# Rows of the scaled layer norm input 272 elements apart instead of 266, and four small tiles placed in the space before the split input

## The chip, the cores and the metric

The kernel runs on one core of a Trainium2 chip. The metric is the device time of one execution in microseconds. Before the change three timed runs took 1718.97, 1721.99 and 1723.23 us, a median of 1721.99 us.

## What is computed

One decoder layer for 256 prompt tokens and 8 sample tokens, which the kernel carries together as 264 columns (`TOK`). Cut to what matters here:

```
z = x @ w_in                                  # 2048 -> mixers and gates
m = sum_k sigmoid(gate_k(x)) * (branch_k @ w_branch[k])
x1 = LN(alpha*x + m @ w_out) * ln1_g + ln1_b
gate, up = split(x1 @ w_ffn_up)               # 2048 -> 2 x 5632
y  = LN(alpha*x1 + (silu(gate) * up) @ w_ffn_down)
```

Everything is float32. Each large product is made from three TensorE matmuls on high and low parts: `w_hi * x_hi`, `w_hi * x_lo` and `w_lo * x_hi`.

## The kernel before

The activations lie transposed: 128 partitions hold one k tile of 128 features, and the 16 k tiles (`KT`) follow each other along the free dimension, each with 264 columns of 4 bytes. A weight chunk is 512 rows by 256 columns of a weight matrix: four k tiles, two output halves, three matmuls each, so 24 matmuls of 128 x 264. SyncE loads chunks into a ring, ScalarE makes the high part (L1252, later L1548), VectorE the low part (L1664, later L2350), and TensorE multiplies. Four chunks (96 matmuls) make a pass over all 2048 features, and a pass yields 256 output features. The matmuls of one chunk take, for each k tile and half, the high rows, the low rows and the high rows again (L790 to L792; in the feed-forward part L1151 to L1153).

The order of the work is written out by hand. `PASSES` lists the passes before the layer norm: the mixer inputs, then for branches 3, 1, 2 and 0 eight gate passes of four chunks, each followed by one chunk of that branch, and eight output passes. All passes but those of the branches, the two of the GLU (which take the GLU's input) and the output passes use the split input `xh`, `xl`: 5040 matmuls. The output passes use `mh`, `ml`: 768 matmuls. Each engine inserts its small work at written chunk numbers, and waits on counts of semaphores.

The first layer norm is not waited for. The first four of the 22 steps of the up projection (`Z_STEPS`, two passes per step) run on the unnormalized input times the gain, `zh` and `zl`, with two more columns (the gain and the bias), so that their matmuls are 266 columns wide: 768 matmuls. VectorE corrects their results in `normal` with these two columns. ScalarE writes `zh` in `z_high` (L1303 to L1308), VectorE writes `zl` in `z_low`. Meanwhile the norm is finished, and the other 18 steps use `x1h`, `x1l`: 3456 matmuls. The down projection uses `hh`, `hl`: 2112 matmuls.

All tiles have addresses written by hand. `base` is a multiple of 32 bytes, and all offsets count from it. `w_split`, `w_hi` and `w_lo` are made of 512 byte pieces at multiples of 512 bytes from `base`. `xh`, `zh` and `x1h` share one region at `at_xh` = 49152, and `xl`, `zl` and `x1l` one at `at_xl` = `at_xh + XW`, each of them `XW` bytes long. `zh` and `x1h` begin at the region's start, `xh` ends at its end. `at_g`, the start of `mh` and of everything placed behind, follows at `at_xl + XW`. `fix` places small tiles one after the other at the end of the memory; `causal` (512 bytes), `pt` (the page table, 256), `sf` (the final S5 state, 128) and `hos` (128) are among them.

Of the kernel before, what the change touches and what calls it, by code (L numbers as in the profile page):

```python
# [7 lines left out]
F32, F32R, I32 = mybir.dt.float32, mybir.dt.float32r, mybir.dt.int32  # L8
# [4 lines left out]
P = 128  # L13
D_MODEL, SEQ, DEC, MIX, HEADS = 2048, 256, 8, 512, 4
PAST, PAGE = 1024, 128
N_PAGES = PAST // PAGE
D_FF = 5632
TOK = SEQ + DEC
KT = D_MODEL // P
MT = MIX // P  # L20
ALPHA = 2.0 ** 0.25
# [2 lines left out]
S5_TILES = 16  # L24
# [203 lines left out]
def trunk(nc, A, O):  # L228
# [3 lines left out]
    def sem(name):  # L232
        if name not in sems:
            sems[name] = ctx.enter_context(nc.semaphore(name))
        return sems[name]
# [38 lines left out]
    base = (nc.sbuf_base + 31) // 32 * 32  # L274
    ZB = MT * TOK * 4
    XB = KT * TOK * 4
    XW = KT * (TOK + 2) * 4
    CB = W * 4
    at_gate = 2 * RING * CB
    at_xh = 3 * RING2 * CB  # L280
    at_xl = at_xh + XW
    at_g = at_xl + XW
    at_z = at_g + 2 * XB
# [4 lines left out]
    def place(name, shape, dt, off):  # L288
        return nc.alloc_sbuf_tensor_at(name, shape, dt, offset=base + off)
# [3 lines left out]
    w_split = place("w_split", [P, RING, 2, W], F32R, 0)  # L293
    gate = place("gate", [P, N_GATE, 2, TOK], F32, at_gate)

# [4 lines left out]

    xh = place("xh", [P, KT, TOK], F32R, at_xh + XW - XB)
    xl = place("xl", [P, KT, TOK], F32R, at_xl + XW - XB)
    zh = place("zh", [P, KT, TOK + 2], F32R, at_xh)
    zl = place("zl", [P, KT, TOK + 2], F32R, at_xl)
    x1h = place("x1h", [P, KT, TOK], F32R, at_xh)
    x1l = place("x1l", [P, KT, TOK], F32R, at_xl)
    x_t = place("x_t", [P, KT, TOK], F32, at_g)
# [35 lines left out]
    def fix(name, shape, dt=F32):  # L343
        n = 4
        for s in shape[1:]:
            n *= s
        t = place(name, shape, dt, off[0])
        off[0] += (n + 31) // 32 * 32
        assert off[0] <= at_keep, (name, off[0], at_keep)
        return t  # L350

    level_mask = fix("level_mask", [P, NL + 1, P], I32)
    causal = fix("causal", [P, P])
    s5p = fix("s5p", [P, 16, S5_TILES])
    lam_t = s5p[:, 2:8, :]
    h0 = fix("h0", [P, 2, S5_TILES, DEC])
# [7 lines left out]
    cum = fix("cum", [HEADS, 2, SEQ])  # L364
    bf = fix("bf", [HEADS, 1])
    pick = fix("pick", [32 + DEC, DEC], F32R)
    pt = fix("pt", [1, DEC * N_PAGES], I32)
    p_diag = place("p_diag", [P, P], F32, off[0])
    q_rows = fix("q_rows", [P, HEADS, DEC, DEC])
    c_rows = fix("c_rows", [32 + HEADS, HEADS, 32], F32R)  # L370
# [4 lines left out]
    osmp = place("osmp", [P, HEADS, DEC], F32, at_rest + 640)  # L375
    lf_hi = place("lf_hi", [HEADS, DEC], F32R, at_rest + 768)
    lf_lo = place("lf_lo", [HEADS, DEC], F32, at_rest + 800)
    sf = fix("sf", [P, 2, S5_TILES])
    hos = fix("hos", [P, 32])


    gsq = place("gsq", [P, MT, TOK], F32, at_merged)
# [81 lines left out]
    def gain_bias(m):  # L464

        return lnv[:, 0:2, 2 * m:2 * m + 2].rearrange("p n t -> p t n")
# [291 lines left out]
    def _(pe):  # L758
# [385 lines left out]
        def products(slot, bank, right_h, right_l, k0, first, last, width=TOK):  # L1144

            for kk in range(CK):
                rh, rl = right_h[:, k0 + kk, :], right_l[:, k0 + kk, :]
                for half in range(2):
                    out = PS[:, bank + half, 0:width]
                    c = slice((kk * 2 + half) * P, (kk * 2 + half) * P + P)  # L1150
                    nc.tensor.matmul(out, w_hi[:, slot, c], rh, start=(first and kk == 0), stop=False)  # L1151
                    nc.tensor.matmul(out, w_hi[:, slot, c], rl, start=False, stop=False)  # L1152
                    ins = nc.tensor.matmul(out, w_lo[:, slot, c], rh, start=False, stop=(last and kk == CK - 1))  # L1153
            ins.then_inc(sem("used2"), 1)
# [13 lines left out]
        def up_chunk(i, j, right_h, right_l, width=TOK):  # L1168
            n, p, kc = C_UP + j, P_UP + j // 4, j % 4
            if kc == 0:  # L1170
                pe.wait_ge(sem(f"evac{p % 2}"), i + p // 2)
            pe.wait_ge(sem("lo2"), i * 8 + (n + 1))
            products(n % RING2, BANK(p), right_h, right_l, CK * kc, kc == 0, kc == 3, width)
# [19 lines left out]
        for m in range(8):  # L1193
            p = P_DOWN + m
            for kc in range(DOWN_CHUNKS):
                n = C_DOWN + m * DOWN_CHUNKS + kc
                if kc == 0:
                    pe.wait_ge(sem(f"evac{p % 2}"), p // 2)
                if m == 0:
                    pe.wait_ge(sem("hl_done"), CK * (kc + 1) // 2)  # L1200
                pe.wait_ge(sem("lo2"), n + 1)
                if (m, kc) == (7, DOWN_CHUNKS - 1):
                    last_products(n % RING2, BANK(p), hh, hl, CK * kc)
                else:
                    products(n % RING2, BANK(p), hh, hl, CK * kc, kc == 0, kc == DOWN_CHUNKS - 1)
                if (m, kc) == (4, 5):
                    layer_pivot(1)
# [28 lines left out]
    def _(act):  # L1236
# [46 lines left out]
        def due(n):  # L1283

            while emptied[0] < len(PASSES) and last_chunk(emptied[0]) <= n - 3:
                evacuate(emptied[0])
                emptied[0] += 1
            while summed[0] < 8 and last_chunk(pass_of("branch", 0, summed[0])) <= n - 4:
                merged_high(summed[0])
                summed[0] += 1  # L1290
            for m in range(7):
                if n == last_chunk(pass_of("out", m, 0)) + (12 if m == 0 else 9 if m == 1 else 6):
                    squares(0, m, xp)
                    z_high(m)
# [8 lines left out]

        def z_high(m):

            for t in (2 * m, 2 * m + 1):
                A_(zh[:, t, 0:TOK], xp[:, t, :], ACT.Copy, scale=lnv[:, 0, t:t + 1])
            A_(zh[:, 2 * m:2 * m + 2, TOK:TOK + 2], gain_bias(m), ACT.Copy).then_inc(sem("z_high"), 1)  # L1308
# [253 lines left out]
        highs(0, 4)  # L1562
        squares(0, 6, xp)
        z_high(6)
        squares(0, 7, xp)
        z_high(7)
        highs(C_UP + 4, C_UP + 7)
        deviation(0)
# [55 lines left out]
        for n in range(C_DOWN + 4, C_DOWN + 8 * DOWN_CHUNKS):  # L1624
            highs(n, n + 1)
            m, kc = divmod(n - C_DOWN, DOWN_CHUNKS)
# [983 lines left out]
```

## Time and profile before

| | before |
|---|---|
| timed runs | 1718.97, 1721.99, 1723.23 us; median 1721.99 |
| span of the profiled execution | 1718.8 us |
| TensorE matmul busy | 1702.9 us, 99% |
| VectorE busy | 1073.3 us, 62% |
| ScalarE busy | 796.3 us, 46% |
| chain that ended last | TensorE 97% |
| DMA | 329.75 MB, mean 192 GB/s |

The profile was taken in one execution. It gives the span from the first to the last instruction; a separate time of that execution is not given. Its span lies 0.2 us under the shortest timed run and 3.2 us under the median. Matmuls overlap in the profile: a matmul's own duration is longer than the distance from its start to the next one's start. That distance, below called the pitch, is what adds up, so stages are compared by the starts of their matmuls.

### The profile page before, as it was taken

What the parts mean: (1) busy time and instruction counts of PE and PEld (TensorE: products, weight loads), DVE (VectorE), ACT (ScalarE), POOL (GpSimd) and SP (SyncE); (2) the same over time, 40 slices, a digit from 0 to 9 for tenths busy, and PEclk for the clock granted to TensorE, in tenths of its full rate; (3) what the DMA queues carried; (4) which work ended last, traced back from release to release, by engine and by line L of the source; (5) the groups of instructions that cost most, each with busy time, mean ns of one, the idle gap of its engine ahead of it and who ended that gap; (6) DMA issues with size and microseconds to landing.
All of it is one profiled execution on the core that took longest, in us unless ns stands there. A gap on an engine that the chain in (4) does not pass through costs nothing.

```text
span 1718.8 us, 33400 instructions
## 1 busy us (share of the span) xinstructions
PE 1702.9 (99%) x13814; PEld 1652.8 (96%) x13814; DVE 1073.3 (62%) x1271; ACT 796.3 (46%) x894; POOL 141.8 (8%) x148
## 2 busy tenths in 40 slices
PE   9999999999999999999999999999999999999998
PEld 8999888999999999999999999999999999999997
DVE  7798887756657666455587784444444444454755
ACT  5654544557444444444454564344444443333433
POOL 8200000000012555000000000000000000000000
PEclk9999999999999999999999999999999999999999
DMA  7565467776647887555555556555555555555552
GB/s 253 161 209 160 148 205 240 233 236 210 213 151 239 283 254 256 184 180 184 175 180 178 178 165 193 182 182 177 179 182 182 176 179 183 184 172 184 183 173 88
DMA packets 309558, 329.75 MB, mean 192 GB/s; under 512 B 12223, under 2 KB 289987, under 8 KB 309188
## 3 DMA queue, kind: packets, MB, share of 16 engines
q1 hardware_dynamic: 308044, 326.59, 59.7%
q8 instruction: 84, 1.38, 0.3%
q10 hardware_dynamic: 1400, 1.54, 0.3%
q14 instruction: 30, 0.25, 0.0%
HBM read 322.31 MB, written 5.77 MB: 191 GB/s over the span
## 4 chain that ended last, share of the span: by engine, by line
PE 97%; DVE 1%; DMA 1%; ACT 0%; issue 0%; SPq 0%; DVEq 0%; ACTq 0%
PE ps L790 15%; PE ps L791 15%; PE ps L1152 15%; PE ps L792 15%; PE ps L1153 15%; PE ps L1151 15%; PE ps L863 1%; PE ps L1040 1%; DMA w_in_ring<-in_w_in 1%; PE ps L898 0%; PE ps L828 0%; PE ps L813 0%; DVE w_split L1664 0%; PE ps L806 0%; PE ps L841 0%
## 5 line engine op out<-in xcount | busy, mean ns | idle before, releaser
L2350 DVE TENSOR_TENSOR w_lo<-w_raw,w_hi 128x1024 fp32r<-128x1024 f32 x264 | 322.8, 1225 | 326.0 <-ACT w_hi L1548 323.0
L1664 DVE TENSOR_TENSOR w_split<-w_in_ring,w_split 128x1024 fp32r<-128x1024 f32 x276 | 346.8, 1259 | 240.6 <-ACT w_split L1252 230.8
L790 PE MATMUL ps<-xh,w_split 128*128 128x264 f32 x1680 | 482.5, 287 | 3.5 <-DVE w_split L1664 3.5
L1548 ACT ACTIVATE w_hi<-w_raw 128x1024 fp32r<-128x1024 f32 x264 | 279.4, 1060 | 439.3 <-PE ps L1153 433.9
L791 PE MATMUL ps<-xl,w_split 128*128 128x264 f32 x1680 | 478.6, 285 | 0.0
L792 PE MATMUL ps<-xh,w_split 128*128 128x264 f32 x1680 | 477.2, 284 | 0.0
L1252 ACT ACTIVATE w_split<-w_in_ring 128x1024 fp32r<-128x1024 f32 x276 | 291.0, 1059 | 357.4 <-DMA w_in_ring<-in_w_in 262.8
L790 PEld LDWEIGHTS ps<-xh,w_split 128*128 128x128 f32 x1680 | 316.6, 188 | 20.7 <-issue 17.3
L1152 PE MATMUL ps<-x1l,w_hi 128*128 128x264 f32 x1152 | 327.6, 284 | 0.0
L1153 PE MATMUL ps<-x1h,w_lo 128*128 128x264 f32 x1152 | 326.8, 284 | 0.0
L1151 PE MATMUL ps<-x1h,w_hi 128*128 128x264 f32 x1152 | 325.8, 283 | 0.0
L792 PEld LDWEIGHTS ps<-xh,w_split 128*128 128x128 f32 x1680 | 316.7, 189 | 0.0
L791 PEld LDWEIGHTS ps<-xl,w_split 128*128 128x128 f32 x1680 | 316.6, 188 | 0.1
L1153 PEld LDWEIGHTS ps<-x1h,w_lo 128*128 128x128 f32 x1152 | 216.7, 188 | 0.0
L1151 PEld LDWEIGHTS ps<-x1h,w_hi 128*128 128x128 f32 x1152 | 216.6, 188 | 0.0
L1152 PEld LDWEIGHTS ps<-x1l,w_hi 128*128 128x128 f32 x1152 | 216.2, 188 | 0.0
L1152 PE MATMUL ps<-hl,w_hi 128*128 128x264 f32 x696 | 198.0, 284 | 0.0
L1153 PE MATMUL ps<-hh,w_lo 128*128 128x264 f32 x696 | 197.4, 284 | 0.0
L1151 PE MATMUL ps<-hh,w_hi 128*128 128x264 f32 x696 | 197.1, 283 | 0.0
L1153 PEld LDWEIGHTS ps<-hh,w_lo 128*128 128x128 f32 x696 | 130.9, 188 | 0.0
L1151 PEld LDWEIGHTS ps<-hh,w_hi 128*128 128x128 f32 x696 | 130.9, 188 | 0.0
L1152 PEld LDWEIGHTS ps<-hl,w_hi 128*128 128x128 f32 x696 | 130.6, 188 | 0.0
(502 smaller groups left out, 2158.1 us busy)
## 6 DMA issues: line engine op xcount, KB each, us to landing
w_in_ring<-in_w_in SPq DMA_DIRECT2D x210, 512.0 KB, 3.5
w_raw<-in_w_ffn_up SPq DMA_DIRECT2D x176, 512.0 KB, 4.4
w_raw<-in_w_ffn_down SPq DMA_DIRECT2D x88, 512.0 KB, 3.2
kv<-in_cache_k SPq DMA_DIRECT2D x64, 258.0 KB, 3.7
w_in_ring<-in_w_branch SPq DMA_DIRECT2D x32, 512.0 KB, 4.3
kv<-in_cache_v SPq DMA_DIRECT2D x64, 256.0 KB, 3.7
w_in_ring<-in_w_out SPq DMA_DIRECT2D x32, 512.0 KB, 3.3
x_t<-in_x SPq DMA_DIRECT2D x8, 264.0 KB, 6.8
```

What stands on the lines that cost most here:

```text
L790: nc.tensor.matmul(out, w_split[:, slot, 0, c], right_h[:, k, :], start=first, stop=False)
L791: nc.tensor.matmul(out, w_split[:, slot, 0, c], right_l[:, k, :], start=False, stop=False)
L792: ins = nc.tensor.matmul(out, w_split[:, slot, 1, c], right_h[:, k, :], start=False, stop=last)
L863: ins = nc.tensor.matmul(PS[32 * h:32 * h + DEC, bank, :].rearrange("p (a t) -> p a t", a=4), q_rows[:, h, b, :], kv[:, u % 2, :, h * P:h ...
L1040: ins = nc.tensor.matmul(out, keys, queries, start=True, stop=True)
L1151: nc.tensor.matmul(out, w_hi[:, slot, c], rh, start=(first and kk == 0), stop=False)
L1152: nc.tensor.matmul(out, w_hi[:, slot, c], rl, start=False, stop=False)
L1153: ins = nc.tensor.matmul(out, w_lo[:, slot, c], rh, start=False, stop=(last and kk == CK - 1))
L1252: A_(w_split[:, n % RING, 0, :], w_in_ring[:, n % RING, 1, :], ACT.Copy).then_inc(sem("hi_done"), 1)
L1548: A_(w_hi[:, n % RING2, :], raw[:, n % RING2, :], ACT.Copy).then_inc(sem("hi2"), 1)
L1664: V.tensor_tensor(w_split[:, slot, 1, :], w_in_ring[:, slot, 1, :], w_split[:, slot, 0, :], ALU.subtract).then_inc(sem("lo_done"), 1)
L2350: V.tensor_tensor(w_lo[:, n % RING2, :], raw[:, n % RING2, :], w_hi[:, n % RING2, :], ALU.subtract).then_inc(sem("lo2"), 1)
```

## The change

The row distance of `zh` and `zl` becomes `ZROW` = 272 elements (1088 bytes) instead of 266 (1064 bytes), and the regions of the split input become 16 x 272 x 4 = 17408 bytes long instead of 17024. The matmuls still read 266 columns, which `products` now says with a slice. `xh` and `xl` still end at the end of their regions; 512 bytes are free before each. `causal` goes into the 512 bytes before `xl`, and `pt`, `sf` and `hos` into the 512 bytes before `xh`. Before the first write to `zh` ScalarE waits until both stores that are counted by `s5_stored` have landed (one of them reads `sf`).

```diff
+ZROW = TOK + 8
-    XW = KT * (TOK + 2) * 4
+    XW = KT * ZROW * 4
-    zh = place("zh", [P, KT, TOK + 2], F32R, at_xh)
-    zl = place("zl", [P, KT, TOK + 2], F32R, at_xl)
+    zh = place("zh", [P, KT, ZROW], F32R, at_xh)
+    zl = place("zl", [P, KT, ZROW], F32R, at_xl)
-    causal = fix("causal", [P, P])
+    causal = place("causal", [P, P], F32, at_xl)
-    pt = fix("pt", [1, DEC * N_PAGES], I32)
+    pt = place("pt", [1, DEC * N_PAGES], I32, at_xh)
-    sf = fix("sf", [P, 2, S5_TILES])
-    hos = fix("hos", [P, 32])
+    sf = place("sf", [P, 2, S5_TILES], F32, at_xh + DEC * N_PAGES * 4)
+    hos = place("hos", [P, 32], F32, at_xh + DEC * N_PAGES * 4 + 2 * S5_TILES * 4)
@@ products
-                rh, rl = right_h[:, k0 + kk, :], right_l[:, k0 + kk, :]
+                rh, rl = right_h[:, k0 + kk, 0:width], right_l[:, k0 + kk, 0:width]
@@ z_high(m)
+            if m == 0:
+                act.wait_ge(sem("s5_stored"), 32)
```

The remainders of the start addresses (offsets from `base`), worked out from the code, for the first k tile of each pair. All rows but those of `zh` and `zl` are 1056 bytes apart, before and after, and each next k tile of these begins 32 bytes further modulo 256.

| high, low | offset modulo 256 before | after |
|---|---|---|
| `xh`, `xl` | 128, 0 | 0, 0 |
| `mh`, `ml` | 0, 0 | 0, 0 |
| `zh`, `zl` | 0, 128 (next: +40) | 0, 0 (next: +64) |
| `x1h`, `x1l` | 0, 128 | 0, 0 |
| `hh`, `hl` | 128, 0 | 128, 0 |

## Rows read from the trace of the kernel before

**Rows 1.** The page: span, busy time, granted clock in 40 slices, chain by engine.
```profile
span 1718.8 us, 33400 instructions
...
PE   9999999999999999999999999999999999999998
...
PEclk9999999999999999999999999999999999999999
...
PE 97%; DVE 1%; DMA 1%; ACT 0%; issue 0%; SPq 0%; DVEq 0%; ACTq 0%
```

**Rows 2.** Groups of matmuls by line and form: busy us, mean ns | idle before.
```profile
L791 PE MATMUL ps<-xl,w_split 128*128 128x264 f32 x1680 | 478.6, 285 | 0.0
...
L1152 PE MATMUL ps<-x1l,w_hi 128*128 128x264 f32 x1152 | 327.6, 284 | 0.0
...
L1151 PE MATMUL ps<-zh,w_hi 128*128 128x266 f32 x256 | 74.2, 290 | 2.0 <-DVE w_lo L2350 2.0
...
L790 PE MATMUL ps<-mh,w_split 128*128 128x264 f32 x256 | 73.1, 286 | 0.5 <-DVE ml L1691 0.5
```

**Rows 3.** TensorE in order of time (start, us): scaled input, five passes apart.
```profile
952.40 0.29 PE L1151 MATMUL ps<-zh,w_hi 128*128 128x266 f32 x1
...
1011.80 0.29 PE L1151 MATMUL ps<-zh,w_hi 128*128 128x266 f32 x1
```

**Rows 4.** The same: first matmul on the normalized input, first of the down projection.
```profile
1023.68 0.28 PE L1151 MATMUL ps<-x1h,w_hi 128*128 128x264 f32 x1
...
1443.20 0.28 PE L1151 MATMUL ps<-hh,w_hi 128*128 128x264 f32 x1
...
1489.84 0.28 PE L1151 MATMUL ps<-hh,w_hi 128*128 128x264 f32 x1
```

**Rows 5.** The same: input projection, two stretches, each one pass of four chunks.
```profile
60.11 0.28 PE L790 MATMUL ps<-xh,w_split 128*128 128x264 f32 x1
...
71.76 0.28 PE L790 MATMUL ps<-xh,w_split 128*128 128x264 f32 x1
...
725.37 0.28 PE L790 MATMUL ps<-xh,w_split 128*128 128x264 f32 x1
...
737.03 0.28 PE L790 MATMUL ps<-bh,w_split 128*128 128x264 f32 x1
```

**Rows 6.** The same: output projection; two chunks, a wait, then four passes.
```profile
827.43 0.28 PE L790 MATMUL ps<-mh,w_split 128*128 128x264 f32 x1
...
833.25 0.28 PE L790 MATMUL ps<-mh,w_split 128*128 128x264 f32 x1
...
836.85 0.39 PE L790 MATMUL ps<-mh,w_split 128*128 128x264 f32 x1 [0.50 <-DVE ml L1691]
...
861.36 0.28 PE L790 MATMUL ps<-mh,w_split 128*128 128x264 f32 x1
...
908.40 0.28 PE L790 MATMUL ps<-mh,w_split 128*128 128x264 f32 x1
```

**Rows 7.** Stretches: us, busy (x) of PE, PEld, DVE, ACT, POOL, PEclk, DMA share, GB/s.
```profile
925.00:935.00 10.00, 9.71 (x66) 9.74 (x67) 8.49 (x12) 3.79 (x6) 0.00 (x0) 0.83 0.68 208
...
975.00:1000.00 25.00, 25.00 (x204) 25.00 (x203) 19.42 (x26) 13.34 (x19) 0.00 (x0) 1.00 0.58 182
```

**Rows 8.** ScalarE in order of time around the first write of `zh`.
```profile
864.88 1.06 ACT L1252 ACTIVATE w_split<-w_in_ring 128x1024 fp32r<-128x1024 f32 x1 [2.86 <-DMA w_in_ring<-in_w_out]
865.85 0.63 ACT L1301 ACTIVATE sqt<-xp 128x528 f32<-128x528 f32 x1
866.60 0.92 ACT L1307 ACTIVATE zh<-xp,lnv 128x264 fp32r<-128x264 f32 x2
```

**Rows 9.** The moved tiles: duration min/median/max, first and last start us.
```profile
L1440 ACTq DMA_DIRECT2D out_s_prompt<-sf x1: 372/372/372, 346.2 to 346.2; - x1
...
DMA to landing us min/median/max: 6.0/6.0/6.0
...
L2316 DVE TENSOR_TENSOR s_sb<-ps,causal x2: 681/682/683, 602.3 to 644.7; 128x512 f32<-128x512 f32 x2
...
L529 SPq TENSOR_LOAD <-pt x128: 263/270/1493, 253.9 to 686.3; - x128
...
L1472 ACT ACTIVATE hf<-hos x1: 230/230/230, 500.9 to 500.9; 128x32 f32<-128x32 f32 x1
```

**Rows 10.** The chain in order of time: eight 128 x 128 transposes (start us, us).
```profile
44.35 0.87 PE ps L806 x8
```

## The prediction

> **What bounds the kernel now.** I read the page first [rows 1]: TensorE carries 97% of the chain that ended last, its matmuls are busy in every slice, and the granted clock is full in practically all of them. So any change of the matmuls' pitch (the distance from one start to the next) goes into the time one for one, and any change on another engine is hidden unless TensorE comes to wait for it. Second, the groups by line and form [rows 2]: durations differ by little (284 to 290 ns for whole stages), but they overlap and are no price. The price is the pitch, so third I read the starts of matmuls at the bounds of passes, where the same number of matmuls lies between two rows.
>
> - Scaled input, 266 columns: 1011.80 - 952.40 = 59.40 us for 20 chunks, five passes, 480 matmuls: 11.88 us a pass, 123.75 ns a matmul [rows 3].
> - Normalized input, 264 columns: 1443.20 - 1023.68 = 419.52 us for 36 passes, 3456 matmuls: 11.653 us a pass, 121.39 ns [rows 4]. The down projection: 46.64 us for 16 chunks, 11.66 us for four [rows 4].
> - Input projection: 71.76 - 60.11 = 11.65 us and 737.03 - 725.37 = 11.66 us a pass [rows 5].
> - Output projection: 908.40 - 861.36 = 47.04 us for four passes: 11.76 us a pass, 122.50 ns [rows 6]. Yet its first two chunks took 833.25 - 827.43 = 5.82 us, 11.64 us for four: it became slower after the wait at 836.85, and from then on stayed so.
>
> The last point decides this case. The output projection has the same matmul form, the same number of columns, the same ring `w_split` as the input projection, and a full clock. What it has alone is where its rows lie: the first high and the first low row both start at a multiple of 256 bytes, and so each high and low row of one k tile have the same remainder modulo 256. In the three stages that run at 11.65 the two are 128 bytes apart modulo 256 (the table of remainders). Nothing else that I find separates 11.76 from 11.65: the load of the other engines and the DMA is as high in the feed-forward stages, which do not pay it.
>
> **The change part by part.**
>
> 1. The scaled input. Its excess over the normalized input is 11.880 - 11.653 = 0.227 us a pass, 1.8 us in all eight passes. Two columns at the full clock are two cycles of 2.4 GHz, 0.83 ns a matmul, 0.08 us a pass; they stay. The rest, 0.147 us a pass, 1.2 us in all, is what the odd starts can cost if rows at 32 byte steps are the measure. But the changed rows have equal remainders for high and low, as `mh`, `ml` have: by the nearest row 11.76 + 0.08 = 11.84 us a pass, a gain of 0.04, times 8 = 0.3 us. I take that, since it is the row with these remainders. Bounds: rows that all start on 64 bytes are not in the trace. Eight transposes, each with 128 columns and a weight load, take 0.87 us, 109 ns each [rows 10], which is what a load costs when the stream is short; 266 columns at one per cycle are 110.8 ns. So no more than 123.75 - 110.8 = 13 ns a matmul, 9.9 us over 768, can go. Above, if equal remainders cost here what they cost at 264 columns (1.1 ns) and the 64 byte starts give nothing, 0.9 us is added.
>
> 2. The input projection. The region grows from 17024 bytes (66.5 times 256) to 17408 (68 times 256), so `xl` lies a whole number of 256 bytes behind `xh`, and both now start at remainder 0: exactly the layout of `mh`, `ml`, with the same weights' ring. The price is 11.76 - 11.653 = 0.107 us a pass, 1.11 ns a matmul. 5040 matmuls are 52.5 passes: 5.6 us at most. The stage has many waits and small products between passes, and a wait is what turned the output projection slow. But its first two chunks, which came right behind a branch 0 chunk with differing remainders, ran at the fast pitch. The seven gate passes behind such chunks may do so too, 28 of 210 chunks. I take the other 182: 182 / 4 x 0.107 = 4.9 us. Bounds: 0 and 5.6 us.
>
> 3. The normalized input. `x1h`, `x1l` come to remainders 0 and 0 as well. 36 passes x 0.107 = 3.8 us. There is no wait in this stage; it inherits the rhythm of the scaled input before it. Bounds: 0 and 3.8 us.
>
> 4. `mh`, `ml`, the branch inputs, `hh`, `hl` all shift by 768 bytes, three times 256: their remainders stay, I count 0.
>
> 5. The wait on `s5_stored`. The store that reads `sf` is issued at 346.2 and lands 6.0 us later; the first write of `zh` is at 866.60 [rows 8, 9], so the wait is met by 514 us. Behind it on ScalarE are two writes of `zh` and the high part of the next chunk. ScalarE had idled 2.86 us just before, for a DMA of weights [rows 8], so even one more ScalarE step of 0.63 us there would be absorbed. If that cover were gone it would cost TensorE those 0.6 us once. No instruction, DMA or queue is moved in order: `pt` is still loaded at the same place on SyncE.
>
> 6. The four tiles change places only. `pt` is last read at 686.3, `causal` at 644.7, `hos` at 500.9 [rows 9], all before `zh` is written. Reads and writes of 128 to 683 ns on engines that wait for TensorE: 0.
>
> 7. The start of the scaled input, with 2.0 us idle and a stretch at granted clock 0.83 on average (full before and after) [rows 2, 7], hangs on ScalarE's and VectorE's steps there, which the change leaves: 0.
>
> Sum: -0.3 + 4.9 + 3.8 = +8.4 us. The profiled span 1718.8 would become 1727.2; it stands 3.2 us under the median, so I forecast 1721.99 + 8.4 = 1730.4 us.
>
> **A rule against this.** The rows show two pitches for matmuls of one form at one clock, 121.4 and 122.5 ns [rows 4, 6]. The Trainium skill, SBUF — State Buffer, says that within the engine side only the port pair that VectorE and GpSimd share causes contention and that TensorE never waits on anyone; TensorE: Matmul & The Clock Gate (the steps of a matmul) adds that TensorE has two independent read ports, one for the moving rows and one for the weights. By that, addresses would not matter, parts 2 and 3 would be 0, and the sum would be that of rival A. No page has a rule on remainders modulo 64 or 256, so the row decides the sum, and the rule is part of rival A's chance.
>
> **The rivals.**
>
> A. Equal remainders are not the cause of 11.76; it belongs to the output projection for a reason that I don't see, or the new stages stay in the fast rhythm. For it: the first two chunks at 5.82 us with the same addresses [rows 6], and one slow stage is one case. Against it: 28 chunks in a row at the slow pitch, through another interruption. Then only part 1 counts: between -0.3 and -1.2 us, 1720.8 to 1721.7, say 1721.2 us. Chance 0.28.
>
> B. Only one of the two large stages takes the slow rhythm. Only the normalized input: +3.8 - 0.3 = 3.5, 1725.5 us; only the input projection: +4.9 - 0.3 = 4.6, 1726.6 us. It decides which whether waits set the rhythm (the first has none). Chance 0.15.
>
> C. The other side: starting on 64 bytes matters much more than the 32 byte rows show, and the pitch of the scaled input falls near its floor. It would have to save over 5.2 us, 6.8 ns of 123.75 on each of 768 matmuls. At 8 ns: 6.1 us, 1715.9 us, with parts 2 and 3 at nothing. Against it: half of the `x1h` rows start on 64 bytes already and the other half 32 bytes off, and the whole stage is at 121.4. Chance 0.03.
>
> D. The change does what it says of addresses (each k tile starts on 64 bytes by the arithmetic: 1088 is 17 times 64), but the pitch does not follow: the scaled input stays at 11.88. With parts 2 and 3 that is 1730.7 us; it stays within my forecast.
>
> **How the numbers follow.** Forecast and D together 0.54, A 0.28, B 0.15, C 0.03. What a measurement of this kernel can tell is about 0.3%, 5.2 us: same is 1716.8 to 1727.2 us. The forecast lies beyond it at 1730.4, and so does its upper bound, 1721.99 + 5.6 + 3.8 + 0.9 = 1732.3; A lies within. B at its upper bound of 5.6 + 0.9 goes a little beyond. So slower 0.55, same 0.41, faster 0.04. The range reaches from A's lower part, 1720.3, to the upper bound with a little spread of the runs, 1733.0.
>
> **What would show it.** Right: the passes of the input projection and of the normalized input at 11.76 us, with the latter stage 423.4 us long instead of 419.5; the scaled input near 11.84 a pass; the output and down projections as before. Step 1 is wrong if a pass of the scaled input is under 11.7. Wrong as a whole: the normalized input still 11.65 a pass, which is rival A. If one stage is at 11.76 and the other at 11.65, it is B. A new idle time of ScalarE at the first write of `zh`, or of TensorE before the scaled input beyond 2.0 us, would show that part 5 or 7 was wrong.

## The result and the profile after

The changed kernel is slower: 1724.77 us median of 11 runs (1722.28 to 1726.68) against 1719.32 us of the kernel before in 11 runs beside it (1718.21 to 1723.55). The ratio is 1.0022, with a 95% interval from 1.0013 to 1.0032: 3.8 us, between 2.2 and 5.5. The medians themselves lie 5.45 us apart. That is the direction forecast, inside the 0.3% that the prediction had called no change, and by the ratio less than half of the 8.4 us forecast.

The page of the changed kernel (span; TensorE's busy time and instructions; granted clock in 40 slices):

```profile
span 1722.6 us, 33400 instructions
...
PE 1707.5 (99%) x13814; PEld 1657.0 (96%) x13814; DVE 1075.5 (62%) x1271; ACT 798.5 (46%) x894; POOL 139.4 (8%) x148
...
PEclk9999999999999999999999999999999999999999
```

The profiled execution took 1724.44 us, 1.8 us over its span. TensorE is as full as before [rows 1]. So the starts of matmuls at the bounds of passes must show where the time went. TensorE of the changed kernel in order of time (start, us); line numbers are one higher than before. First the normalized input, the starts of its first six chunks, and the start of the down projection:

```profile
1023.69 0.28 PE L1152 MATMUL ps<-x1h,w_hi 128*128 128x264 f32 x1
...
1026.58 0.29 PE L1152 MATMUL ps<-x1h,w_hi 128*128 128x264 f32 x1
...
1029.50 0.28 PE L1152 MATMUL ps<-x1h,w_hi 128*128 128x264 f32 x1
...
1032.44 0.28 PE L1152 MATMUL ps<-x1h,w_hi 128*128 128x264 f32 x1
...
1035.39 0.28 PE L1152 MATMUL ps<-x1h,w_hi 128*128 128x264 f32 x1
...
1038.32 0.28 PE L1152 MATMUL ps<-x1h,w_hi 128*128 128x264 f32 x1
...
1446.99 0.28 PE L1152 MATMUL ps<-hh,w_hi 128*128 128x264 f32 x1
...
1493.63 0.28 PE L1152 MATMUL ps<-hh,w_hi 128*128 128x264 f32 x1
```

The stage takes 1446.99 - 1023.69 = 423.30 us where it took 419.52 [rows 4]: 11.758 us a pass instead of 11.653, 3.8 us in all. The reader should also look at the first chunks: 2.89, 2.92, 2.94, 2.95, 2.93 us. Before the change the chunks of this stage take 2.91 and 2.92 us in turn, and in the changed kernel the later ones 2.93 and 2.95 us. So the first two chunks do not pay, the first is even 0.02 us shorter than before, and the third pays in full. The down projection, whose remainders did not change, keeps its 46.64 us for 16 chunks [rows 4].

Scaled input (five passes), output projection (four passes), a gate pass behind a branch 0 chunk, and the first matmul of the output projection:

```profile
952.49 0.28 PE L1152 MATMUL ps<-zh,w_hi 128*128 128x266 f32 x1
...
1011.82 0.28 PE L1152 MATMUL ps<-zh,w_hi 128*128 128x266 f32 x1
...
864.41 0.28 PE L791 MATMUL ps<-mh,w_split 128*128 128x264 f32 x1
...
911.45 0.28 PE L791 MATMUL ps<-mh,w_split 128*128 128x264 f32 x1
...
725.00 0.28 PE L791 MATMUL ps<-xh,w_split 128*128 128x264 f32 x1
...
736.71 0.28 PE L791 MATMUL ps<-bh,w_split 128*128 128x264 f32 x1
...
827.48 0.28 PE L791 MATMUL ps<-mh,w_split 128*128 128x264 f32 x1
```

The scaled input takes 59.33 us for five passes, 11.867 us each instead of 11.880 [rows 3]: the aim of the change brings 0.1 us over eight passes. The output projection stays at 47.04 us for four [rows 6]. The gate pass went from 11.66 [rows 5] to 11.71 us. From the chunk that began at 60.11 us before [rows 5], the 16th of the trace, and that begins at 58.39 us now, up to the output projection, the input projection took 827.43 - 60.11 = 767.32 us before and 827.48 - 58.39 = 769.09 us now: 1.8 us more. That the spans differ by only 3.8 us, though these stages add 1.8 + 3.8 - 0.1 = 5.5 us, has its reason at the start, below.

ScalarE at the first write of `zh`, where the new wait stands, shows no idle time of the wait's: the write starts at 866.81 right behind the square, as it did before [rows 8].

```profile
866.07 0.62 ACT L1302 ACTIVATE sqt<-xp 128x528 f32<-128x528 f32 x1
866.81 0.92 ACT L1310 ACTIVATE zh<-xp,lnv 128x264 fp32r<-128x264 f32 x2
```

### The profile page after: what moved, and what is told of

Read it like the earlier page. It is cut to its first block, busy times and chain, and to the rows that moved or that the text cites. A ratio compares the mean times of both kernels' runs of the same rounds, so it can differ in the third digit from the quotient of the medians.

```text
span 1722.6 us, 33400 instructions
## 1 busy us (share of the span) xinstructions
PE 1707.5 (99%) x13814; PEld 1657.0 (96%) x13814; DVE 1075.5 (62%) x1271; ACT 798.5 (46%) x894; POOL 139.4 (8%) x148
## 4 chain that ended last, share of the span: by engine, by line
PE 94%; POOL 1%; DVE 1%; DMA 1%; ACT 1%; SPq 1%; issue 0%; DVEq 0%; POOLq 0%; ACTq 0%
PE ps L1153 15%; PE ps L1152 15%; PE ps L1154 15%; PE ps L791 15%; PE ps L792 14%; PE ps L793 14%; PE ps L864 1%; PE ps L1041 1%; DMA w_in_ring<-in_w_in 1%; POOL v_sum L754 1%; POOL kv L750 1%; PE ps L829 0%; DVE w_split L1667 0%; PE ps L814 0%; DMA kv<-in_cache_v 0%
```

## The experiments

All runs start from the changed kernel. Where a run was timed once, its time says little, since the times of one kernel spread over 5 us and more; its stages decide. The theory was that of the prediction: the distance between the high and the low row of a k tile modulo 256 bytes sets the pitch.

**The region of the low rows 128 bytes further on.** Rows of `zh` and `zl` stay 272 apart, the four small tiles stay moved, the wait stays.

```diff
-    at_xl = at_xh + XW
+    at_xl = at_xh + XW + 128
```

> The changed kernel with the second region 128 bytes further on: high and low rows of xh/xl, zh/zl and x1h/x1l again 128 bytes apart modulo 256, zh and zl still 272 elements per row. Theory (the distance of high and low rows modulo 256 sets the pitch): input projection and normalized input back at 11.65 us a pass (normalized stage 419.5 us instead of 423.3), output projection unchanged at 11.76; total 3.8 + about 2.3 us under the changed kernel, level with the kernel before within 1.5 us. Scaled input: 11.73 us a pass if its excess was the same cause, 11.87 if not. Rival (the scaled input's 1088 byte rows leave a slower rhythm behind, or the four moved tiles cost): the normalized input stays at 11.76 and the total at that of the changed kernel.

Measured: 1719.32 us median of 12 runs, ratio to the kernel before, with 23 runs beside it, 0.9995 (0.9984 to 1.0006). Its starts at the bounds of five passes of the scaled input and of the normalized stage:

```profile
949.99 0.29 PE L1152 MATMUL ps<-zh,w_hi 128*128 128x266 f32 x1
...
1009.19 0.29 PE L1152 MATMUL ps<-zh,w_hi 128*128 128x266 f32 x1
...
1021.03 0.28 PE L1152 MATMUL ps<-x1h,w_hi 128*128 128x264 f32 x1
...
1440.55 0.28 PE L1152 MATMUL ps<-hh,w_hi 128*128 128x264 f32 x1
```

The normalized stage takes 419.52 us, to the hundredth what it took before. The scaled input takes 59.20 us for five passes, 11.840 us each: between the two values expected, and 0.04 us under the kernel before. The input projection, from the like chunk on, takes 766.89 us against 767.32 before. By the stages the whole loss is gone with 128 bytes of distance, so neither the moved tiles, nor the wait, nor the 1088 byte rows had caused any of it.

**The same, and `ml` 128 bytes further on.** What lies behind `ml` moves with it (the lines for `hh`, `hl` and the tiles behind them are left out below).

```diff
-    at_xl = at_xh + XW
+    at_xl = at_xh + XW + 128
-    at_z = at_g + 2 * XB
+    at_z = at_g + 2 * XB + 128
-    ml = place("ml", [P, KT, TOK], F32R, at_g + XB)
+    ml = place("ml", [P, KT, TOK], F32R, at_g + XB + 128)
```

> As the run before, and ml also 128 bytes further on, so that mh and ml are 128 apart modulo 256 as well. Theory: the output projection falls from 11.76 to 11.65 us a pass, about 0.6 to 0.7 us over its seven slow passes, all else as in the run before; total some 0.7 us under it, too little for the timed runs alone. Rival (the output projection is slow for a reason of its own, such as the wait at its third chunk): 11.76 stays.

Measured: 1718.90 us median of 11 runs, ratio 0.9988 (0.9977 to 0.9999). The output projection, four passes:

```profile
862.31 0.28 PE L791 MATMUL ps<-mh,w_split 128*128 128x264 f32 x1
...
908.93 0.28 PE L791 MATMUL ps<-mh,w_split 128*128 128x264 f32 x1
```

46.62 us instead of 47.04, 11.655 us a pass. A stage that the change had never touched is made faster by 128 bytes, by 0.10 us a pass and 0.6 us over the stage (97.24 us from its first matmul to the scaled input's, against 97.86 before). Its own slowness had been the remainders too, and nothing in its waits. Its median is the lowest of all the kernels, 0.4 us under the one before it, which the timed runs can't tell from nothing; its interval only just leaves out no change against the kernel before. Its profiled span, 1714.6 us, is not to be compared as it stands: it had the full clock at the start of the scaled input (see below).

**Only the input projection's rows apart.**

```diff
-    at_xl = at_xh + XW
-    at_g = at_xl + XW
+    at_xl = at_xh + XW + 128
+    at_g = at_xl + XW + 128
-    zl = place("zl", [P, KT, ZROW], F32R, at_xl)
+    zl = place("zl", [P, KT, ZROW], F32R, at_xl + 128)
-    x1l = place("x1l", [P, KT, TOK], F32R, at_xl)
+    x1l = place("x1l", [P, KT, TOK], F32R, at_xl + 128)
```

> Only xh and xl are 128 apart modulo 256; zh/zl and x1h/x1l keep equal remainders. Theory: undisturbed passes of the input projection 11.65 us, normalized input 11.76 us (stage 423.3 us). Rival (the stage before sets the rhythm of those after it, the layout does not): both at one pitch.

Measured, one run: 1726.16 us. A gate pass, and the bounds of the normalized stage:

```profile
723.01 0.28 PE L791 MATMUL ps<-xh,w_split 128*128 128x264 f32 x1
...
734.67 0.28 PE L791 MATMUL ps<-bh,w_split 128*128 128x264 f32 x1
...
1021.32 0.28 PE L1152 MATMUL ps<-x1h,w_hi 128*128 128x264 f32 x1
...
1444.61 0.28 PE L1152 MATMUL ps<-hh,w_hi 128*128 128x264 f32 x1
```

The gate pass is back at 11.66 us, the normalized stage takes 423.29 us. In one kernel each stage goes by its own remainders.

**Rows of 266 elements again, regions long.**

```diff
-    zh = place("zh", [P, KT, ZROW], F32R, at_xh)
-    zl = place("zl", [P, KT, ZROW], F32R, at_xl)
+    zh = place("zh", [P, KT, TOK + 2], F32R, at_xh)
+    zl = place("zl", [P, KT, TOK + 2], F32R, at_xl)
```

> The changed kernel with zh and zl rows again 266 elements apart, in the same longer regions, so with high and low at equal remainders. Theory: normalized input and input projection as in the changed kernel (11.76 us steady); the scaled input between 11.84 and 12.0 us a pass, since it now has odd starts and equal remainders. Rival (the 1088 byte rows cause the slower stages): the normalized input falls to 11.65 us.

```profile
953.00 0.28 PE L1152 MATMUL ps<-zh,w_hi 128*128 128x266 f32 x1
...
1012.50 0.28 PE L1152 MATMUL ps<-zh,w_hi 128*128 128x266 f32 x1
```

One run, 1724.97 us. The scaled input takes 59.50 us for five passes, 11.900 each; the normalized stage 423.30 us. So the four cases of the scaled input are known:

| us a pass | low 128 from high | at the same remainder |
|---|---|---|
| rows 1064 bytes apart | 11.880 (before) | 11.900 |
| rows 1088 bytes apart | 11.840 | 11.867 (the change) |

The rows of 1088 bytes are worth 0.03 to 0.04 us a pass, 0.3 us in all eight, and equal remainders take back 0.02 to 0.03 of it. Whether the start on a multiple of 64 bytes does it, or that the rows go through the remainders in other steps, these runs don't tell apart (the offsets count from `base`, a multiple of 32 bytes).

**Other distances, and another place against the weights.** Three kernels with 32, 64 and 192 in place of the 128 of the first edit, and one in which everything from `xh` on lies 128 bytes further while high and low keep equal remainders (`at_xh = 3 * RING2 * CB + 128`).

> The changed kernel with the low region 64 bytes further on: high and low rows 64 apart modulo 256 in the input projection, the scaled and the normalized input. Theory (their distance modulo 256 sets the pitch): all other stages as in the changed kernel; the normalized input between 11.65 and 11.76 us a pass, or above if 0 is not the worst distance. Rival (any distance but 0 is free): 11.65.

> The same with 32 bytes. By the theory near the 11.76 us of distance 0 if the cost falls off with distance; 11.65 by the rival that only exact equality costs.

> The same with 192 bytes (64 short of 256). If only the distance to the nearest multiple of 256 counts, the pitch of the run with 64 bytes; if direction counts too, another one.

> The changed kernel with everything from xh on 128 bytes further: high and low rows at equal remainders, both 128 where they were 0, so half a period further against the weights. Theory (only the distance of high to low counts, over a whole pass that goes through all remainders): normalized input and output projection again 11.76 us a pass. Rival (the place against the weights counts, and remainder 0 was the bad one): 11.65 us.

One run each, 1722.21, 1722.38, 1723.69 and 1727.28 us. The bounds of the normalized stage with 32, 64 and 192, and behind them those of the scaled input's five passes with 192:

```profile
1022.25 0.28 PE L1152 MATMUL ps<-x1h,w_hi 128*128 128x264 f32 x1
...
1443.20 0.28 PE L1152 MATMUL ps<-hh,w_hi 128*128 128x264 f32 x1
```

```profile
1022.57 0.29 PE L1152 MATMUL ps<-x1h,w_hi 128*128 128x264 f32 x1
...
1443.08 0.29 PE L1152 MATMUL ps<-hh,w_hi 128*128 128x264 f32 x1
```

```profile
1024.06 0.28 PE L1152 MATMUL ps<-x1h,w_hi 128*128 128x264 f32 x1
...
1445.96 0.28 PE L1152 MATMUL ps<-hh,w_hi 128*128 128x264 f32 x1
...
952.54 0.28 PE L1152 MATMUL ps<-zh,w_hi 128*128 128x266 f32 x1
...
1012.14 0.28 PE L1152 MATMUL ps<-zh,w_hi 128*128 128x266 f32 x1
```

The normalized stage with all 128 further: its first four chunks and its end.

```profile
1022.78 0.28 PE L1152 MATMUL ps<-x1h,w_hi 128*128 128x264 f32 x1
...
1025.69 0.28 PE L1152 MATMUL ps<-x1h,w_hi 128*128 128x264 f32 x1
...
1028.63 0.28 PE L1152 MATMUL ps<-x1h,w_hi 128*128 128x264 f32 x1
...
1031.58 0.28 PE L1152 MATMUL ps<-x1h,w_hi 128*128 128x264 f32 x1
...
1446.11 0.28 PE L1152 MATMUL ps<-hh,w_hi 128*128 128x264 f32 x1
```

The normalized stage of 36 passes, worked out from the first matmul on `x1h` and on `hh` in each:

| low behind high, modulo 256 | stage, us | us a pass |
|---|---|---|
| 0 (the change) | 423.30 | 11.758 |
| 0, all 128 further | 423.33 | 11.759 |
| 32 | 420.96 | 11.693 |
| 64 | 420.51 | 11.681 |
| 128 | 419.52 | 11.653 |
| 192 | 421.90 | 11.720 |

In this stage the cost is greatest at 0 and smallest at 128, falls off on both sides, and is not symmetric: 192 costs more than 64, so it is not the distance to the nearest multiple of 256 alone. The rival that only exact equality costs falls (32 costs 0.04 us a pass). The rival that the place against the weights counts falls too for a whole pass, since moving both by 128 changes the stage by 0.03 us only; the output projection keeps its 47.04 us for four passes there.

The other stages do not follow the same curve. The scaled input's five passes take 59.33 us with 32 and with 64, as with 0, and 59.60 us with 192, more than with equal remainders. The input projection takes 769.1, 768.5 and 769.3 us with 32, 64 and 192: about what it takes with 0. In all three stages 128 is the least. No run shows what else shapes the curve.

What the place does change is where the slow rhythm sets in. With all rows 128 bytes further the second chunk pays already: 2.91, then 2.94 and 2.95 us. The six matmuls of one k tile show it more exactly. In the changed kernel the 4th k tile of the stage takes 723 ns and the 12th, with the same remainder of 96, takes 752 ns. With all rows 128 further the 8th has that remainder, and takes 753 ns.

**An interruption before each pass.** One 128 x 128 matmul of constants more, before each of 34 passes of the normalized input, in the changed kernel and in the one with regions 128 apart. The trace shows each of them as two TensorE instructions.

```diff
             for j in range(8):
+                if j % 4 == 0:
+                    nc.tensor.matmul(PS[:, 7, 0:P], ones[:, :], ident[:, :], start=True, stop=True)
                 up_chunk(i, j, x1h, x1l)
```

> The changed kernel with one extra 128 x 128 float32 matmul of constants, whose result is not used, before each of the 34 passes of the last 17 steps on the normalized input. Theory (the slow rhythm of equal remainders needs about three chunks to build up behind an interruption, and this is why the input projection, with its small products and branch chunks, pays only about half): the four chunks behind each extra matmul take about 2.90, 2.92, 2.94 and 2.95 us instead of 2.949 and 2.931 in turn, 11.71 us for the four beyond what the extra matmul itself costs. Rival (the input projection pays less because waits for weights hide it; a TensorE that never waits pays all): the pass keeps 11.76 us beside the cost of the extra matmul.

> The same extra matmuls in the layout with the regions 128 bytes apart modulo 256. Theory: the pass takes 11.66 us beside the extra matmul's own cost, so that the two layouts differ by about 0.05 us a pass, half of the 0.107 us without interruptions. Rival: they still differ by 0.107 us.

One run each, 1728.42 and 1727.75 us. The starts of the four chunks of a pass and of the next pass, first with equal remainders, then 128 apart:

```profile
1069.72 0.37 PE L1152 MATMUL ps<-x1h,w_hi 128*128 128x264 f32 x1
...
1072.69 0.29 PE L1152 MATMUL ps<-x1h,w_hi 128*128 128x264 f32 x1
...
1075.61 0.28 PE L1152 MATMUL ps<-x1h,w_hi 128*128 128x264 f32 x1
...
1078.55 0.28 PE L1152 MATMUL ps<-x1h,w_hi 128*128 128x264 f32 x1
...
1081.64 0.37 PE L1152 MATMUL ps<-x1h,w_hi 128*128 128x264 f32 x1
```

```profile
1068.81 0.37 PE L1152 MATMUL ps<-x1h,w_hi 128*128 128x264 f32 x1
...
1071.80 0.28 PE L1152 MATMUL ps<-x1h,w_hi 128*128 128x264 f32 x1
...
1074.72 0.28 PE L1152 MATMUL ps<-x1h,w_hi 128*128 128x264 f32 x1
...
1077.63 0.28 PE L1152 MATMUL ps<-x1h,w_hi 128*128 128x264 f32 x1
...
1080.69 0.37 PE L1152 MATMUL ps<-x1h,w_hi 128*128 128x264 f32 x1
```

A pass with its extra matmul takes 11.92 us with equal remainders and 11.88 us with 128 apart: they differ by 0.04 us where they differ by 0.105 without interruption. The first chunk is 0.02 us shorter with equal remainders (2.97 against 2.99), the second takes 2.92 us in both, the third 2.94 against 2.91, and the fourth, with the extra matmul behind it, 3.09 against 3.06. The extra matmul costs the layouts different amounts: 0.16 us of the pass in the one (11.92 - 11.76), 0.23 in the other (11.88 - 11.65). No waits are added, so the rival that waits for weights hide the cost is not needed; an interruption by itself takes away more than half of it. Not every interruption does. In the output projection of the changed kernel four matmul instructions of another kind (L814) stand before the chunk at 858.34, and the second chunk behind them, from 861.46 to 864.41, takes 2.95 us, the slow rhythm in full; with `mh` and `ml` 128 apart it takes 2.91.

```profile
861.46 0.28 PE L791 MATMUL ps<-mh,w_split 128*128 128x264 f32 x1
```

## Why the prediction was wrong

The mechanism was right: in all stages whose high and low rows got equal remainders the pitch rose, and it went back when they were set apart. One term was mis-sized.

- Part 1, scaled input: forecast 11.84 us a pass and a gain of 0.3 us, measured 11.867 and 0.1 us. Small, and with the right sign. The 109 ns that it sets beside its lower bound are a misreading: the eight records of [rows 10] are four transposes, since each call on 128 x 128 float32 leaves two (as the extra matmuls do: 68 for 34), so one takes 218 ns and not 109. The sum does not use them.
- **Part 2, input projection: the failed step.** The prediction took 182 of 210 chunks at the steady slow pitch, 4.9 us. Measured are 1.8 us between the like chunks of the two profiles. The same stretch took on average 767.2 us in the five kernels with 128 bytes of distance (766.9 to 767.4) and 769.3 us in the four with equal remainders (769.0 to 769.7): 2.1 us. That the output projection "became slower after the wait" put the cause at the wait, and was misread: its first two chunks were fast because the slow rhythm had not set in yet. The first two of the normalized input show the same (2.89 and 2.92 us), without a wait.
  In the input projection nearly every pass is followed by a branch chunk or a small product, and the stream begins anew. Worked out from the starts of its 195 chunks from the 16th of the trace on, by the median of the five kernels at 128 bytes against the median of three with equal remainders (the changed one, the one with rows of 266, the one with extra matmuls), for the chunks that nothing interrupts: the first behind a break costs 9 ns less, the second 9 ns more on average (most of them nothing, some 31), the third and the fourth 30 ns each, the few later ones 27. Of the 195 chunks 66 stand third or later; if those that something interrupts pay alike, that makes 2.0 us, near the 2.1 measured. So the price per chunk was about right, 27 ns in the prediction, and the number of chunks that pay it was not. The row that could have told it stood in the prediction: 5.82 us for two chunks.
- Part 3, normalized input: forecast 3.8, measured 3.8 us.
- Part 4: `mh`, `ml` and `hh`, `hl` at 47.04 us for four passes and 46.64 us for 16 chunks, as before. Right.
- Parts 5 and 6, the wait and the moved tiles: nothing, as forecast; the kernel with 128 bytes of distance keeps them all and is level with the kernel before.
- Part 7: right; the 2.0 us idle before the scaled input is there again. The stretch at a lower clock behind it belongs to the execution and not to the kernel, though: 6 of the 12 traces have it, among them those of both kernels here, and 6 have the full clock there. With equal layouts of these rows, the stage from the first matmul on `zh` to the first on `x1h` takes 98.31 us with it (the changed kernel) and 96.79 us without (all 128 further).

With 2.1 in place of 4.9 us and -0.1 in place of -0.3 the sum is 5.8 us, a little above the measured interval; by the profile's own stages, 1.8, 3.8 and -0.1, it is 5.5, its upper end. A second error has nothing to do with the change: the forecast time started from 1721.99 us, the median of three runs, and the median of 11 is 1719.32.

The two spans differ by 3.8 us because of the start: of the kernel before the first chunk took 4.43 us, of the changed one 2.99 us. The stretch from 3 to 15 us of both, before and then after (us, busy (x) of TensorE, weight load, VectorE, ScalarE and GpSimd, granted clock, DMA share, GB/s):

```profile
3.00:15.00 12.00, 9.89 (x36) 6.63 (x35) 6.42 (x8) 6.70 (x9) 9.39 (x21) 0.86 1.04 354
```

```profile
3.00:15.00 12.00, 10.64 (x53) 7.31 (x52) 6.90 (x8) 7.28 (x10) 9.39 (x21) 1.00 1.04 353
```

At a mean of 0.86 over 12 us the kernel before ran some 3.4 us of it at half clock (12 x 0.14 / 0.5), the changed one none. Both kernels do the same there, and the kernels with 266 element rows and with extra matmuls 128 apart show the slow start again (their first chunks took 4.30 and 4.21 us, at a mean of 0.86 and 0.87), so it belongs to the single execution. Such stretches are worth some 1.5 us each, which is why two spans must be compared stage by stage. The timed runs bear it out, for they come with a mean granted clock (only the 11 of the kernel before, beside the changed one, do not). Of the kernel before, in the 23 runs taken beside the experiments, those at 0.998 took 1717.5 us on average, at 0.997 1719.1, at 0.996 1720.3, and at 0.995 and 0.994 1722.9 and 1723.0. The changed kernel took 1723.0 us at 0.998, 1724.7 at 0.997 and 1726.1 at 0.996. So at the same granted clock the two kernels differ by 5.5 to 5.8 us, which is what the stages add up to; the 3.8 us of the ratio are also shaped by how often each kernel met such stretches. The runs are few at each level and come from two sets, so this supports the stages and is no measurement of its own.

Rival A (no cost of remainders) is refuted by four kernels, and the rule of two independent read ports that the prediction set beside it (the Trainium skill, TensorE: Matmul & The Clock Gate) does not tell what these runs show: the pitch depends on the place of the rows. Rival B came near the total (1725.5 us) for a wrong reason: both stages pay, one of them in part. No run shows what it is in the chip that makes the pitch go by the remainder, why some interruptions reset it and others not, or why it sets in at one k tile and not another; that stays open.

## What to carry to other kernels

When a tile's size changes, the tiles behind it move, and streams that are read in turn change their distance to each other: before and after, tabulate the start addresses of the operands that alternate, modulo 256 bytes, for all stages and not only for the one that is meant. Where TensorE is full all the time and alternates between two equally strided arrays, put them 128 bytes apart modulo 256; here it was worth up to 0.1 us in 11.7, least in the stage with other row lengths, and it can be tried with a single constant. Before comparing two spans or a few timed runs, look at the granted clock of each. Price a steady effect by the length of the undisturbed streams, not by the count of instructions.

## What was not expected of the hardware

- The pitch of one and the same matmul form goes from 121.4 ns with high and low rows 128 bytes apart modulo 256 to 122.5 ns with 0, with values between at 32, 64 and 192.
- The slow rhythm sets in some chunks of 24 matmuls after the stream began: with the third when the rows start at remainder 0 (2.89, 2.92, 2.94, 2.95 us), with the second when they start at 128 (2.91, 2.94, 2.95 us). One extra matmul before each pass makes it begin anew (the two layouts then differ by 0.04 us a pass instead of 0.105), but four matmul instructions in the output projection did not.
- Rows of 1088 bytes instead of 1064, with 266 columns, are worth 0.04 us in 11.88 at the most.
- The first chunk behind a break is 0.02 us shorter with equal remainders than with 128 bytes between (2.97 against 2.99 us).
